# A hybrid attention step on one core: the order in which attention takes its query tiles

## The chip, the core and the metric

The kernel runs on one core of a Trainium2 chip. The core has a matrix engine (TensorE, PE in the profile), a vector engine (VectorE, DVE), a scalar engine (ScalarE, ACT), a general engine (GpSimd, POOL) and a queue engine (SyncE, SP) that issues most transfers (DMA). Each runs its own list of instructions in order and waits on semaphores for the others. [...] The metric is device time in microseconds (us); lower is better.

## The reference, cut to what matters

One layer reads 1024 prompt rows, 64 sample rows and 16 meta rows, all 1024 wide. After a normalisation and one input projection, two attentions run side by side, A over a sliding window and B over the keys that an indexer selects; both are gated, summed, and followed by an output projection and an MLP.

```python
o_a = swa_prompt(qa, ka, va, mk_a, mv_a, attn_sinks, slopes_a)      # branch A: window of 128, whole 64-row chunks
o_b = dsa_prompt(qb, qi, wi, kb, vb, ki, mk_b, mv_b, slopes_b, n)   # branch B: top 256 of all earlier keys
mix = (sigmoid(g_a) * o_a + sigmoid(g_b) * o_b) @ w_o
x = x + rms_norm(mix, g_post_mix)
hid = square(relu(rms_norm(x, g_pre_mlp) @ w_up))
y = x + rms_norm(hid @ w_down, g_post_mlp)
```

Each query row is independent of the others once the keys, values and selections are there, so the order of the query rows is free.

## The kernel before

The program runs in stages with a barrier between them: normalisation and projection (to about 616 us of the span), attention (about 617 to 1103), output projection (to about 1235), MLP (to the end). Queries, gates, the distance masks of branch B and the merged rows pass through scratch tensors in memory.

Attention takes nine query tiles: 0 to 7 are 128 prompt rows each, 8 (`SAMPLE_TILE`) is the 64 sample rows. `ORDER` is the order of the tiles. A tile has two sections, branch A then branch B (`SECTIONS`), a section has two blocks of 64 rows (the sample one), and a block has eight units, one for each pair of heads. So a prompt section has 16 units and a sample section 8. In this text 7A is branch A of tile 7, 0B branch B of tile 0, and SA and SB are the sample's two sections.

The key columns of a unit depend on branch and block (`key_columns`). Branch A: 80 for block 0, 144 for block 1, 208 for every other block and for the sample. Branch B: 80 and 144 for tile 0, 208 and 272 for tile 1, then 64 more for each block, 976 and 1040 for tile 7, and 1104 for the sample. The columns are cut into key tiles of 128; the last is ragged (16 or 80 rows in B, and 17 or 81 in A, where the sink is one column more).

TensorE goes through the units in a software pipeline. In step u it transposes unit u-2 (L1432), computes the scores of unit u+1 (L1418: two passes, the high and low part of the keys) and multiplies unit u-3 by the values (L1446). VectorE adds the distances and finds the minimum (L1357), ScalarE takes the exponential (L1317), both copy the transposes (L1311, L1369), and VectorE normalises four units at a time (L1376, L1383).

The queries of section s+1 are split into a high and a low part by GpSimd (`split_queries`, L1266 and L1269) once section s-1 has been scored and the queries have landed; only section 0 is split by ScalarE and VectorE. SP issues in order: the queries of the first two sections (L1186), the masks of the first two blocks (L1195), their gates (L1203), thirteen output copies (L1218), and then in a loop over the sections the queries two sections ahead, the masks, the stores of merged rows (L1208), the gates and a piece of `w_o` (L1250). Since all loops run over `SECTIONS`, `BLOCK_ORDER` and `ALL`, every engine's list follows `ORDER`.

Of the kernel before, what the change touches and what calls it, by code (L numbers as in the profile page):

```python
# [22 lines left out]
SAMPLE_TILE = 8  # L23
# [1023 lines left out]
def attention(nc, top, c, ps, kv, wo_raw, wo_loaded, w_o, q_scr, gate_scr, dist_scr, merged_scr, t_scr, caches, outs):  # L1047


    with ExitStack() as ctx:  # L1050
        sb = lambda n, s, d=F32: ctx.enter_context(nc.sbuf_tensor(n, s, d))
        sem = lambda n: top.enter_context(nc.semaphore(n))

        ORDER = list(range(SAMPLE_TILE - 1, -1, -1)) + [SAMPLE_TILE]
        SECTIONS = [(t, branch) for t in ORDER for branch in range(2)]
        halves = lambda t: 2 if t < SAMPLE_TILE else 1
        BLOCK_ORDER = [(t, e) for t in ORDER for e in range(halves(t))]
        block_index = {at: i for i, at in enumerate(BLOCK_ORDER)}
# [116 lines left out]
        with nc.Block() as block:  # L1175

            @block.sync
            def _(sp):
# [55 lines left out]
                for s in range(len(SECTIONS)):  # L1234
# [3 lines left out]
                    if branch == 0:  # L1238
                        mine = [i for i, (t, _) in enumerate(BLOCK_ORDER) if t == ORDER[j]]
                        if j >= 1:  # L1240
# [17 lines left out]
            def _(pool):  # L1258
# [13 lines left out]
                def gate_a(i):  # L1272

                    pool.wait_ge(normed, last_quad[i, 0] + 1)
                    pool.wait_ge(gates_loaded[i % 2], 32 * (i // 2 + 1))
                    if i >= 2:
                        pool.wait_ge(merged_stored[i % 2], 32 * (i // 2))
                    pool.tensor_tensor(merged[:, i % 2], mixed[:, 0, i % 2], gates[:, i % 2, 0], ALU.mult).then_inc(gated_a, 1)
                    pool.wait_ge(gated_a, i + 1)
# [9 lines left out]
                for s in range(len(SECTIONS)):  # L1289
# [6 lines left out]
                    if branch == 1:  # L1296
                        for e in range(halves(ORDER[j])):
                            gate_a(2 * j + e)
# [690 lines left out]
def streaming_step(nc, a, o):  # L1989
# [9 lines left out]
    with ExitStack() as top:  # L1999
# [9 lines left out]
        with ExitStack() as mixers:  # L2009
            ctx = ExitStack()  # L2010
            xT = [ctx.enter_context(nc.sbuf_tensor(n, [P, KT, N_TOK], F32R)) for n in ("xT_hi", "xT_lo")]
            b2 = weight_buffers(ctx, nc, weights)
            input_norm(nc, top, c, xT, b2, ws, ps, a["w_in"], a["x_prompt"], a["x_sample"], a["meta_tokens"], a["g_pre_mix"])
            b2 |= projection_buffers(ctx, nc)
            sel = selection_buffers(ctx, nc)


            ctx.close()
            kv = attention_buffers(mixers, top, nc)
            with ExitStack() as ctx:  # L2020
                raw = operand_buffers(ctx, nc)
                projection(nc, top, c, xT, b2, ws, sel, kv, raw, ps, a["w_in"], caches, a["cache_ki_b"], a["attn_sinks"],
                           t_scr, q_scr, gate_scr, dist_scr)
            attention(nc, top, c, ps, kv, wo_raw, wo_loaded, a["w_o"], q_scr, gate_scr, dist_scr, merged_scr, t_scr, caches, o)
# [35 lines left out]
```

## Time and profile before

| | us |
|---|---|
| median of 3 runs | 2064.34 (2063.37 to 2066.57) |
| the profiled execution | 2057.04 |
| its span, first to last instruction | 2055.2 |
| TensorE busy | 1936.7 (94%) |
| VectorE, ScalarE, GpSimd busy | 1185.1, 715.9, 577.3 |
| mean granted clock of TensorE | 0.965 |

The times within the trace are microseconds from the start of the span. The profiled execution lies 1.84 us above its span and 7.30 us below the median of the runs. [...]

### The profile page before, as it was taken

The numbers are of one execution on the slowest core, as the hardware profiler recorded it, in microseconds if no ns is written. First come the engines' busy times: TensorE is split into PE (matmuls) and PEld (weight loads), VectorE is DVE, ScalarE is ACT, GpSimd is POOL, SyncE is SP. The second block draws the span as 40 slices with busy tenths as digits, with TensorE's granted clock in tenths as the row PEclk, the third lists the DMA queues.
The fourth block names the chain that finished last, engine by engine and source line by source line (L and its number), as shares of the span: only waits on it lengthen the run. The fifth ranks groups of instructions, "written<-read, shape, count | busy, mean of one in ns | idle before, by whom it ended". The sixth has DMA issues, their size and how long they took to land. (4 is left out here: it accounts for less than half of the span.)

```text
span 2055.2 us, 31223 instructions
## 1 busy us (share of the span) xinstructions
PE 1936.7 (94%) x11175; PEld 1745.9 (85%) x11175; DVE 1185.1 (58%) x2717; ACT 715.9 (35%) x1408; POOL 577.3 (28%) x444
## 2 busy tenths in 40 slices
PE   4999999999957999999997998999999999999995
PEld 3989999877747999999997877888888888888884
DVE  6028999999885576667754653333333333333337
ACT  5235444233224555556544333111121212121222
POOL 2225554233123123333631002222222222222224
PEclk9999999999976999999968998999999999999998
DMA  5333333333149044445432323111111111111104
GB/s 150 109 84 98 93 94 86 90 101 89 44 110 175 24 85 97 89 89 97 86 75 98 123 82 98 42 41 41 41 41 41 46 41 46 41 46 41 54 12 153
DMA packets 141257, 158.99 MB, mean 77 GB/s; under 512 B 28320, under 2 KB 109296, under 8 KB 141152
## 3 DMA queue, kind: packets, MB, share of 16 engines
q1 hardware_dynamic: 127328, 136.88, 25.2%
q10 hardware_dynamic: 13824, 20.75, 4.3%
q8 instruction: 62, 1.02, 0.2%
q14 instruction: 43, 0.35, 0.1%
HBM read 119.44 MB, written 39.27 MB: 77 GB/s over the span
## 5 line engine op out<-in xcount | busy, mean ns | idle before, releaser
L1962 PE MATMUL ps<-x2T_hi,weights 128*128 128x362 f32 (+1 forms) x1536 | 383.1, 329 | 5.3 <-DVE weights L1928 5.3
L1980 PE MATMUL ps<-weights,hid_hi 128*128 128x512 f32 (+1 forms) x1152 | 363.0, 396 | 0.0
L1913 DVE TENSOR_TENSOR total<-total,ps 128x512 f32<-128x512 f32 (+1 forms) x270 | 184.6, 686 | 164.4 <-PE ps L1980 163.5
L1962 PEld LDWEIGHTS ps<-x2T_hi,weights 128*128 128x128 f32 x1536 | 273.4, 189 | 7.0 <-DVE weights L1928 5.5
L1980 PEld LDWEIGHTS ps<-weights,hid_hi 128*128 128x128 f32 (+1 forms) x1152 | 209.6, 182 | 57.0
L1962 PE MATMUL ps<-x2T_lo,weights 128*128 128x362 f32 (+1 forms) x768 | 252.7, 329 | 0.0
L1898 DVE TENSOR_TENSOR hidden<-hidden 128x362 f32<-128x362 f32 (+1 forms) x96 | 51.5, 537 | 310.7 <-ACT hidden L1871 310.7
L1980 PE MATMUL ps<-weights,hid_lo 128*128 128x512 f32 (+1 forms) x576 | 228.1, 396 | 0.0
L722 DVE MATCH_REPLACE8 score<-top,score 128x1024 f32<-128x1024 f32 (+6 forms) x224 | 207.2, 929 | 0.0
L718 DVE MAX8 top<-score 128x8 f32<-128x1024 f32 (+6 forms) x224 | 203.0, 936 | 1.9
L1831 POOL TENSOR_TENSOR weights<-down_raw,weights 128x512 fp32r<-128x512 f32 x64 | 82.8, 1294 | 419.2 <-ACT weights L1862 419.2
L1317 ACT ACTIVATE probs<-probs,neg 128x209 f32<-128x209 f32 (+19 forms) x272 | 168.8, 622 | 14.3 <-DVE neg L1357 12.1
L1311 ACT ACTIVATE pt<-ps 128x512 f32<-128x512 f32 (+3 forms) x224 | 104.6, 489 | 197.1 <-PE ps L1432 196.7
L1446 PE MATMUL ps<-v_b_p,pt 128*128 128x65 f32 (+2 forms) x1280 | 172.9, 278 | 0.0
L1446 PEld LDWEIGHTS ps<-v_b_p,pt 128*128 128x128 f32 (+2 forms) x1280 | 166.8, 196 | 5.7
L1823 POOL TENSOR_TENSOR weights<-up_raw,weights 128x256 fp32r<-128x256 f32 x124 | 88.2, 747 | 287.7 <-ACT weights L1853 287.7
L1432 PE MATMUL ps<-ident,probs 128*128 128x128 f32 (+2 forms) x976 | 164.5, 288 | 0.2 <-ACT probs L1317 0.2
L782 PE MATMUL ps<-xT_hi,w_hi 128*128 128x362 f32 (+1 forms) x480 | 159.0, 331 | 0.0
L782 PE MATMUL ps<-xT_hi,weights 128*128 128x362 f32 (+1 forms) x480 | 157.6, 328 | 0.0
L782 PE MATMUL ps<-xT_lo,w_hi 128*128 128x362 f32 (+1 forms) x480 | 157.2, 328 | 0.0
L1862 ACT ACTIVATE weights<-down_raw 128x512 fp32r<-128x512 f32 x64 | 40.1, 626 | 318.4 <-PE ps L1980 318.3
L591 POOL TENSOR_TENSOR weights<-w_raw,w_hi 128x512 fp32r<-128x512 f32 x72 | 93.4, 1297 | 200.4 <-ACT w_hi L497 200.2
(189 smaller groups left out, 3604.7 us busy)
## 6 DMA issues: line engine op xcount, KB each, us to landing
w_raw<-in_w_in ACTq DMA_DIRECT2D x72, 256.0 KB, 2.9
q_raw<-q_scr SPq DMA_DIRECT2D x32, 512.0 KB, 8.5
up_raw<-in_w_up SPq DMA_DIRECT2D x64, 256.0 KB, 2.9
down_raw<-in_w_down SPq DMA_DIRECT2D x64, 256.0 KB, 2.6
gates<-gate_scr SPq DMA_DIRECT2D x34, 256.0 KB, 4.7
x_in<-in_x_prompt SPq DMA_DIRECT2D x16, 512.0 KB, 4.8
gate_scr<-stage SPq DMA_DIRECT2D x32, 256.0 KB, 3.0
q_scr<-stage SPq DMA_DIRECT2D x40, 181.0 KB, 3.1
```

The source lines that it names most:

```text
L591: pool.tensor_tensor(w_lo[:, ch % 2, k, 0:w], w_raw[:, n % RAW, 0:w], w_hi[:, ch % 2, k, 0:w].bitcast(F32), ALU.subtract).then_inc(w_lo_do ...
L718: dve.max(top8[:tile_rows(INDEX_TILES[i]), i % 2], works[i]).then_inc(select_step[i % 2], 1)
L722: dve.match_replace(works[i], top8[:tile_rows(INDEX_TILES[i]), i % 2], works[i], TAKEN)\
L782: last = pe.matmul(out, a, b, start=(k == 0 and j == 0), stop=(k == KT - 1 and j == 2))
L1311: act.activation(pt[:, u % PT, a:a + n, :], src, ACT.Copy).then_inc(copied_act, 1)
L1317: act.activation(probs[:, u % 3, 0:w], probs[:, u % 3, 0:w], ACT.Exp, bias=neg[:, branch, h:h + 1], scale=-1.0).then_inc(exped, 1)
L1432: last = pe.transpose(ps[0:rows, T_BANK + x % 3, b * P:(b + 1) * P], probs[:, u % 3, col:col + rows], c["ident"][:])
L1446: last = pe.matmul(out_bank(q)[:, a, :], pt[0:rows, u % PT, j, :], values(u, j, rows), start=(j == 0), stop=(j == len(tiles) - 1))
L1823: pool.tensor_tensor(up_lo[:, k, :], up_raw[:, k // 2, k % 2, :], up_hi[:, k, :].bitcast(F32), ALU.subtract).then_inc(up_lo_done, 1)
L1913: dve.tensor_tensor(out, out, ps[:r, UP_BANKS + g % DOWN_BANKS, :], ALU.add).then_inc(added, 1)
L1962: last = pe.matmul(ps[:, g % UP_BANKS, 0:n], a[:, k, fs], b, start=(k == 0 and i == 0), stop=(k == KT - 1 and i == 2))
L1980: last = pe.matmul(ps[:r, UP_BANKS + g % DOWN_BANKS, :], a, b[:, f, cols], start=(f == 0 and i == 0), stop=(f == FT - 1 and i == 2))
```

## The change

One line changes: tiles 0 and 1 go first, then 7 down to 2, then the sample.

```diff
-        ORDER = list(range(SAMPLE_TILE - 1, -1, -1)) + [SAMPLE_TILE]
+        ORDER = [0, 1] + list(range(SAMPLE_TILE - 1, 1, -1)) + [SAMPLE_TILE]
```

The sections were 7A 7B 6A 6B ... 2A 2B 1A 1B 0A 0B SA SB, and are 0A 0B 1A 1B 7A 7B ... 2A 2B SA SB. No instruction is added or removed.

TensorE at the start of attention, before (L1418 scores, L1432 transposes by `ident`, L1446 values):

```order
L1404 UNCONDITIONAL_BRANCH
L1418 MATMUL ps<-k_a_p,q_st 128x208 x6
L1432 MATMUL ps<-ident,probs 128x128
L1432 MATMUL ps<-ident,probs 81x128
L1418 MATMUL ps<-k_a_p,q_st 128x208 x2
```

TensorE at the same place, after:

```order
L1404 UNCONDITIONAL_BRANCH
L1418 MATMUL ps<-k_a_p,q_st 128x80 x6
L1432 MATMUL ps<-ident,probs 81x128
L1418 MATMUL ps<-k_a_p,q_st 128x80 x2
L1432 MATMUL ps<-ident,probs 81x128
```

The first units now have 80 key columns and one key tile where they had 208 and two.

TensorE where the sample begins (`k_a_s` are its keys of branch A), before:

```order
L1418 MATMUL ps<-k_b_p,q_st 128x144 x2
L1446 MATMUL ps<-v_b_p,pt 128x65 x2
L1432 MATMUL ps<-ident,probs 128x128
L1432 MATMUL ps<-ident,probs 16x128
L1418 MATMUL ps<-k_a_s,q_st 128x208 x2
```

TensorE where the sample begins, after:

```order
L1418 MATMUL ps<-k_b_p,q_st 128x400 x2
L1446 MATMUL ps<-v_b_p,pt 128x65 x4
L1432 MATMUL ps<-ident,probs 128x128 x3
L1432 MATMUL ps<-ident,probs 16x128
L1418 MATMUL ps<-k_a_s,q_st 128x208 x2
```

The sample now follows the second block of tile 2 (400 columns, four key tiles) where it followed that of tile 0.

SP after the thirteen output copies, in the change from before (-) to after (+); the rows above this piece are the queries of sections 2 and 3:

```order
 L1186 DMA q_raw<-q_scr 64x16x128 x4
+L1195 DMA dist_b<-dist_scr 64x208 x2
+L1195 DMA dist_b<-dist_scr 64x272 x2
+L1208 DMA merged_scr<-merged 64x512 x4
+L1203 DMA gates<-gate_scr 64x1024 x4
+L1250 DMA wo_raw<-in_w_o 64x1024 x2
+L1186 DMA q_raw<-q_scr 64x16x128 x4
+L1195 DMA dist_b<-dist_scr 64x976 x2
+L1195 DMA dist_b<-dist_scr 64x1040 x2
```

The masks of tile 1 are loaded where those of tile 6 stood; all transfers keep their kind and their place in the loop.

## Rows read from the trace of the kernel before

**Rows 1.** The page: 40 slices of the span, TensorE busy and its granted clock.

```profile
PE   4999999999957999999997998999999999999995
PEclk9999999999976999999968998999999999999998
```

**Rows 2.** Stretches of attention, all engines: length, busy time, clock, DMA.

```profile
core 0: us, PE busy (x) PEld busy (x) DVE busy (x) ACT busy (x) POOL busy (x), PEclk, DMA share, GB/s
630.36:655.37 25.01, 24.76 (x118) 24.20 (x119) 14.73 (x64) 9.43 (x23) 8.26 (x3) 0.50 0.92 191
657.00:980.88 323.88, 323.88 (x2688) 314.37 (x2687) 211.74 (x767) 186.45 (x339) 109.52 (x54) 1.00 0.43 81
980.88:997.91 17.03, 17.03 (x151) 16.38 (x149) 13.73 (x62) 9.51 (x24) 10.59 (x7) 1.00 0.40 94
997.91:1014.66 16.75, 16.75 (x146) 15.90 (x144) 12.59 (x51) 11.03 (x26) 9.62 (x5) 1.00 0.88 138
1014.66:1029.64 14.98, 14.66 (x117) 13.25 (x115) 11.59 (x64) 8.07 (x25) 11.21 (x7) 1.00 0.29 63
1032.30:1050.91 18.61, 18.61 (x87) 16.78 (x86) 8.46 (x43) 6.96 (x21) 3.86 (x5) 0.50 0.51 97
1050.91:1065.23 14.32, 14.32 (x66) 13.22 (x65) 7.20 (x32) 4.67 (x12) 7.40 (x5) 0.50 0.19 44
1065.23:1101.00 35.77, 35.30 (x286) 34.23 (x284) 19.70 (x65) 18.31 (x26) 1.27 (x1) 0.98 0.05 13
```

**Rows 3.** Waits of TensorE from 640 to 1101: total, times, longest.

```profile
PE ps L1418 <- DVE neg L1357: 0.4, 2, 0.2
PE ps L1446 <- ACT pt L1311: 0.2, 1, 0.2
```

**Rows 4.** Stretches, score matmuls (L1418) alone, two for each unit: length, busy, clock.

```profile
634.97:649.37 14.40, 6.61 (x18) 4.91 (x19) 0.50 0.78 167
988.43:997.07 8.64, 4.54 (x20) 3.02 (x21) 1.00 0.61 144
998.75:1004.08 5.33, 2.72 (x12) 1.81 (x13) 1.00 1.13 198
1010.21:1013.17 2.96, 0.99 (x4) 0.59 (x5) 1.00 0.04 6
1020.07:1022.91 2.84, 2.00 (x10) 1.50 (x11) 1.00 0.00 0
1026.27:1028.51 2.24, 0.85 (x4) 0.60 (x5) 1.00 0.81 145
1035.84:1038.72 2.88, 1.88 (x6) 1.64 (x7) 0.50 1.10 143
1044.97:1050.90 5.93, 2.04 (x6) 1.64 (x7) 0.50 0.01 3
```

**Rows 5.** Timeline of TensorE where the clock rises: start, length, instruction.

```profile
655.37 1.87 PE L1418 MATMUL ps<-k_b_p,q_st 128*128 128x488 f32 x4
657.61 1.13 PE L1418 MATMUL ps<-k_b_p,q_st 128*128 128x488 f32 x4
...
1065.23 1.85 PE L1418 MATMUL ps<-k_b_s,q_st 128*128 128x368 f32 x6
...
1072.55 1.34 PE L1418 MATMUL ps<-k_b_s,q_st 128*128 128x368 f32 x6
```

**Rows 6.** Stretches at the end of projection, where TensorE only transposes keys.

```profile
605.30:608.90 3.60, 3.58 (x16) 3.27 (x17) 1.54 (x3) 0.75 (x1) 0.00 (x0) 0.50 0.27 51
609.20:611.10 1.90, 1.90 (x17) 1.74 (x16) 1.31 (x3) 0.20 (x1) 0.00 (x0) 1.00 0.61 136
```

**Rows 7.** Timelines of GpSimd and SP at the start of attention.

```profile
645.07 1.36 SPq L1186 DMA_DIRECT2D q_raw<-q_scr  x2
...
653.52 1.89 POOL L1266 CAST q_st<-q_raw 128x2048 fp32r<-128x2048 f32 x1 [15.19 <-DMA q_raw<-q_scr]
655.49 4.58 POOL L1269 TENSOR_TENSOR q_st<-q_raw,q_st 64x2048 fp32r<-64x2048 f32 x1
```

## The prediction, made before the changed kernel had run

> **What bounds the kernel now.** I first read the page's 40 slices [rows 1]. TensorE is nine tenths busy in nearly all of them, and its clock is full except in three places. Slices 12 to 14 and 21 to 22 are the two ends of attention, where the change acts. I then cut attention into stretches by the first score of each section [rows 2]. From 657 to 1101 TensorE has work in the pipeline almost without a gap, and the list of its waits there sums to 0.6 us [rows 3]. VectorE is busy for 12 to 15 us of each prompt section of 15 to 17, ScalarE and GpSimd less. So attention costs what TensorE's instructions cost, and these are the same before and after. The order can only change two things: at which clock each section runs, and whether something arrives late.
>
> The reader is to see the clock column of [rows 2]. It is 0.50 in 7A (630.36 to 655.37), 1.00 from 657 on through 1A, 1B and 0A, 0.50 from 1032.30 through most of 0B and all of SA, and full again in SB. In 7A TensorE is marked busy for 24.76 of 25.01 us, so it is not idleness that keeps the clock low there, and at 1032.30 the clock fell although there was no gap in the rows. The work is what differs. Prompt sections of branch A with 208 columns stay at whichever level they find: 7A at the low one for 25 us, 1A at the high one for 17 [rows 2]. Only the dense score runs of a wide branch B lift the clock: four matmuls of 488 columns at 655.37 and six of 368 at 1065.23, both of which started slow and were followed by fast ones (1.87 us, then 1.13; 1.85 us, then 1.34) [rows 5].
>
> **What one unit costs at either clock** [rows 4]. A stretch there holds a whole number of pipeline steps, two score matmuls each.
> - 208 columns (two key tiles): low clock 14.40 / 9 = 1.60 us; high clock 8.64 / 10 = 0.864 in branch A and 5.33 / 6 = 0.888 in branch B.
> - 80 columns (one tile): low 2.88 / 3 = 0.96; high 2.84 / 5 = 0.57.
> - 144 columns (one tile and a ragged one): low 5.93 / 3 = 1.98; high 2.24 / 2 = 1.12.
> - 272 columns (two tiles and a ragged one): high 2.96 / 2 = 1.48. The low clock isn't shown. From below it is the 1.98 of one tile less, from above twice 1.48 = 2.96. I take 1.98 plus the step from one tile to two at the low clock (1.60 - 0.96 = 0.64), so 2.62.
> The low price of 80 and 144 columns was seen in 0B, and I use it for 0A too, where the second branch-A unit differs by one column (81, 145).
>
> **The change part by part.** The start is as now: SP issues the same queries first, TensorE begins at about 630 at the low clock. What follows now is 0A, 0B, 1A, 1B, 7A, and the first dense score run comes with 7B. So I expect the low clock from the start to the beginning of 7B.
> - 0A moves from the high to the low clock: 8 x (0.96 - 0.57) + 8 x (1.98 - 1.12) = 3.1 + 6.9 = +10.0.
> - 0B was low in all but its first 2.7 us and stays low. The values of 0A's last units trail into those microseconds, and I have charged them to 0A. Nothing more: 0.
> - 1A moves to the low clock: 16 x (1.60 - 0.864) = +11.8.
> - 1B moves to the low clock: 8 x (1.60 - 0.888) + 8 x (2.62 - 1.48) = 5.7 + 9.1 = +14.8. By the bounds of the 272-column step the second part is 8 x (1.98 - 1.48) = 4.0 to 8 x (2.96 - 1.48) = 11.8.
> - 7A was low and stays low: 0.
> - SA now follows the 400-column block of tile 2 at the high clock, as 1A did before, and so stays high: 8 x (0.864 - 1.60) = -5.9. If it fell to the low clock all the same, this term would be 0.
> - SB's first score run is fast: 1.34 - 1.85 = -0.5.
> - The pipeline fills with narrower units: at most 1.60 - 0.96 = 0.64, I take -0.5.
> - 7B's first microseconds: the rise came 1.5 us after its first dense run began, and may come later at another moment. Between 0 and +1.6; I take +0.5.
>
> Sum: 10.0 + 11.8 + 14.8 - 5.9 - 0.5 - 0.5 + 0.5 = +30.2. The profiled execution would go from 2057.0 to 2087.2. The runs' median is 7.3 above the profiled execution for before, and I carry the same difference: 2064.3 + 30.2 = 2094.5.
>
> **What could arrive late.** The queries of 1A are section 2's, and their load is issued behind the thirteen output copies, at 645.07; GpSimd begins their split at 653.52 and is done at 655.49 + 4.58 = 660.07 [rows 7]. Its condition, the scores of section 0 done, comes at about the same time in the new order: 630.4 + 8 x 0.96 + 8 x 1.98 = 653.9. 1A is wanted at about 630.4 + 2 x 23.5 = 677.4, so 17 us remain. For each later section GpSimd begins the split when the section before last has been scored, and needs 6.5 us where the shortest section lasts 23.5. The masks of tiles 0 and 1 are narrower than those of tile 7, so fewer bytes are moved at the start. The stores of tile 0 and the gates of tile 1 stand in front of section 5's queries in SP's list, and those are needed only after 1A and 1B, two sections later. I cost all of it at nothing. What hides it is the slower clock itself; if one section's queries did come late, each microsecond would be one of an idle TensorE.
>
> [...] The row shows 7A at 0.50 for 25.01 us with TensorE busy throughout [rows 2]. [...] A second row shows TensorE with nothing but transposes of keys: 16 in 3.60 us at 0.50, and right after them 17 in 1.90 us at 1.00 [rows 6]. [...]
>
> **The rivals.**
> 1. *The clock rises at the start of 1A*, when the 208-column units follow the small ones. Then 1A and 1B cost what they do now, 7A becomes fast, and only 0A is charged: 10.0 - 11.8 (7A, 16 x 0.736) - 5.9 - 0.5 - 0.5 = -8.7, so 2055.6, faster than before. It decides if 1A differs for the clock from 7A, which has units of the same form and stayed low for all 16. Nothing speaks for it but the alignment of the moment. 5 in 100.
> 2. *The clock rises in 1B*, with the 272-column block or a little before. At the start of 1B: -8.7 + 11.8 = +3.1 (2067.4); at its second block: +5.7 more, +8.8 (2073.1). For it: 272 columns is the widest run before 7A. Against it: such a step has 544 score columns in 2.62 us, and a 208 step 416 in 1.60, so at the low clock it is the thinner one. 7 in 100.
> 3. [...] 3 in 100.
> 4. *The queries or gates come late*. The split of section 2 has 17 us to spare; beyond them each microsecond adds one to the 30.2. With a wait of 5 to 10 us: 2100 to 2105. 4 in 100.
> 5. *The order doesn't matter*, because SA falls to the low clock and something I don't see lifts it in 1A: within a few microseconds of before. 1 in 100.
>
> **How the numbers follow.** My forecast has 80 in 100. Its own range: the 272-column step gives -5.1 to +2.7, the rise in 7B -0.5 to +1.1, and the runs of before lie within 3.2 us of each other, so about 2088 to 2101. For 8 times in 10 I go from 2085 to 2102, which takes in the low end of the 272-column step with some error of the measurement, and leaves out the rivals 1 to 3. A measurement of this kernel can tell about 0.2%, 4 us, from no change. Faster by more: rivals 1 and 3, 0.08. Within it: half of rival 2 and rival 5, 0.05. Slower: the rest, 0.87.
>
> **What would show it.** The stretches of the changed profile should have the clock at 0.50 from about 630 to about 763 (630.4 + 23.5 + 23.5 + 25.6 + 12.8 + 21.0 + 25.6 = 762.4), and at 1.00 without a break from there to the end of SB. Attention should end about 30 us later, at some 1131 instead of 1101, and output projection and MLP should be shifted but not changed. Steps of 80, 144 and 208 columns should have the low prices named, and the first rows of 272 columns at the low clock should be 2.6 us apart. The forecast is wrong if the clock is at 1.00 anywhere before 7B, if SA is at 0.50, or if TensorE has a wait of more than a microsecond on queries (L1269) or masks after its first score.

## The result: 0.3% slower, where 1.5% slower was forecast

| | us |
|---|---|
| changed kernel, median of 12 runs | 2069.52 (2065.84 to 2071.8) |
| before, median of 12 runs beside it | 2064.14 (2055.53 to 2066.57) |
| ratio | 1.0032, 95% interval 1.0019 to 1.0046 |
| forecast | 2094.5, range 2085 to 2102 |

The sign was right. The rise forecast was +30.2 us and the medians differ by 5.4. The changed kernel's profiled execution took 2069.63 us (span 2067.9), against 2057.04 for the one of before: +12.6. That these two differences are not the same is half of the story below.

The slices of the changed kernel's page answer to [rows 1]:

```profile
PE   4999999999958999999997997999999999999995
PEclk7999999999975599999998998999999999999998
```

The low clock at the end of attention is gone, and the one at its start is longer. The same cut by first scores as in [rows 2], with the columns named there, for 0A, 0B, 1A, then 1B in three pieces, 7A, and at the end 2B and SA:

```profile
629.98:648.45 18.47, 18.46 (x85) 17.00 (x85) 10.83 (x60) 7.72 (x23) 6.42 (x2) 0.50 0.89 179
648.45:671.88 23.43, 23.43 (x106) 20.96 (x105) 10.08 (x49) 7.96 (x24) 10.07 (x5) 0.50 0.67 113
671.88:699.01 27.13, 27.13 (x131) 26.03 (x129) 14.45 (x64) 9.53 (x24) 11.06 (x7) 0.50 0.62 122
699.01:711.81 12.80, 12.80 (x67) 12.63 (x65) 6.19 (x25) 4.78 (x13) 8.26 (x4) 0.50 0.48 84
711.81:717.40 5.59, 5.59 (x29) 5.46 (x28) 2.84 (x10) 1.65 (x5) 0.00 (x0) 0.50 0.35 90
717.50:724.24 6.74, 6.74 (x53) 6.10 (x52) 4.08 (x15) 3.83 (x9) 0.83 (x1) 0.98 0.01 2
724.24:740.17 15.93, 15.93 (x142) 15.28 (x139) 13.52 (x62) 9.53 (x24) 10.94 (x7) 1.00 0.36 84
1044.40:1066.59 22.19, 22.19 (x183) 21.53 (x182) 15.63 (x52) 13.48 (x26) 6.83 (x6) 1.00 0.39 77
1066.59:1076.68 10.09, 10.09 (x88) 9.51 (x85) 7.16 (x30) 4.44 (x12) 7.41 (x5) 1.00 0.13 28
```

The clock is 0.50 through 0A, 0B, 1A and the first block of 1B, as forecast, and SA is at full clock (10.09 us, 14.32 before), as forecast. But it rises at 717.8, in the second block of 1B (0.50 up to there, 0.98 as the mean of the stretch from 717.50), and 7A runs at full clock. The steps there show what was overlooked. TensorE's timeline of the changed kernel (start, length, instruction):

```profile
711.81 0.80 PE L1418 MATMUL ps<-k_b_p,q_st 128*128 128x272 f32 x2
712.40 0.95 PE L1446 MATMUL ps<-v_b_p,pt 128*128 128x65 f32 x4
713.15 0.63 PE L1432 MATMUL ps<-ident,probs 128*128 128x128 f32 x2
713.43 0.80 PE L1418 MATMUL ps<-k_b_p,q_st 128*128 128x272 f32 x2
...
715.06 0.80 PE L1418 MATMUL ps<-k_b_p,q_st 128*128 128x272 f32 x2
715.66 0.95 PE L1446 MATMUL ps<-v_b_p,pt 128*128 128x65 f32 x4
716.40 0.84 PE L1432 MATMUL ps<-ident,probs 128*128 128x128 f32 x3
716.90 0.80 PE L1418 MATMUL ps<-k_b_p,q_st 128*128 128x272 f32 x2
717.50 0.70 PE L1446 MATMUL ps<-v_b_p,pt 128*128 128x65 f32 x4
718.03 0.50 PE L1432 MATMUL ps<-ident,probs 128*128 128x128 f32 x3
718.29 0.51 PE L1418 MATMUL ps<-k_b_p,q_st 128*128 128x272 f32 x2
```

The scores run ahead: in the first two steps of the block there are 272 score columns and still the transposes and values of the 208-column units, with two key tiles. Such a step takes 713.43 - 711.81 = 1.62 us. The third has three transposes but still the values of two tiles, and takes 716.90 - 715.06 = 1.84 us. The clock rose in the fourth. The forecast had the first rows of 272 columns 2.6 us apart, the price of a full step, and called that step the thinner one.

Nothing came late. The changed kernel's waits of TensorE from 640 to 1112 answer to [rows 3], and GpSimd had 1A's queries split at 656.04, 15.8 us before 1A's first score (17 forecast; [rows 7]):

```profile
PE ps L1418 <- DVE neg L1357: 0.4, 2, 0.2
PE ps L1418 <- DVE neg_part L1357: 0.2, 1, 0.2
```

```profile
649.56 1.90 POOL L1266 CAST q_st<-q_raw 128x2048 fp32r<-128x2048 f32 x1 [11.69 <-DMA q_raw<-q_scr]
651.53 4.51 POOL L1269 TENSOR_TENSOR q_st<-q_raw,q_st 64x2048 fp32r<-64x2048 f32 x1
```

### The profile page after: what moved, and what is told of

Its sections match the earlier page's. It is cut to its first block and busy times, and to the rows that moved or that the text cites. A ratio compares the mean times of both kernels' runs of the same rounds, so it can differ in the third digit from the quotient of the medians.

```text
span 2067.9 us, 31223 instructions
## 1 busy us (share of the span) xinstructions
PE 1950.1 (94%) x11175; PEld 1758.0 (85%) x11175; DVE 1187.2 (57%) x2717; ACT 716.2 (35%) x1408; POOL 577.7 (28%) x444
## 5 line engine op out<-in xcount | busy, mean ns | idle before, releaser
L1446 PE MATMUL ps<-v_b_p,pt 128*128 128x65 f32 (+2 forms) x1280 | 175.5, 281 | 0.0
L1446 PEld LDWEIGHTS ps<-v_b_p,pt 128*128 128x128 f32 (+2 forms) x1280 | 170.2, 199 | 5.6
L1432 PE MATMUL ps<-ident,probs 128*128 128x128 f32 (+3 forms) x976 | 168.8, 293 | 0.0
```

The source lines that it names most:

```text
L1432: last = pe.transpose(ps[0:rows, T_BANK + x % 3, b * P:(b + 1) * P], probs[:, u % 3, col:col + rows], c["ident"][:])
L1446: last = pe.matmul(out_bank(q)[:, a, :], pt[0:rows, u % PT, j, :], values(u, j, rows), start=(j == 0), stop=(j == len(tiles) - 1))
```

## The experiments

Two theories stood at first. C: all of the difference is TensorE's clock. M: the new order, or the runs of before that take longer than its profile, cost in another way. In 12 runs, 9 of before took 2063 to 2067 us and 3 took 2055 to 2057, and its profile was one of the short ones.

### The kernel before, profiled twice more

No edit.

> The kernel before, unchanged, for a second profile. Its first profile took 2057.0 us, while 9 of 12 runs of it took about 2064 and 3 about 2056. Theory C (all of it is TensorE's clock, and the clock does not fall at the same place in every run): a run of about 2064 has 20 us or so more at granted clock 0.50 in attention than the first profile, by an earlier fall in 1B or 0A (before 1032), since a microsecond at the low clock costs about 0.4. Rival M (the 8 us lie in the MLP or in the projection): attention is as in the first profile, 470.6 us from its first score to 1101, and another stage is longer.

> The kernel before, unchanged, once more. Its times come in groups of about 2044, 2056 and 2065. Theory C: the group follows from two independent events, whether the clock rises early in 7A (low for 25 us or for about 6) and whether it falls early in 0A (near the first 80-column units) or only in 0B. A run of about 2065 has both losses: 7A at 0.50 for 25 us and the fall at the start of 0A; 2044 has neither; about 2056 has one. Rival M: a run of 2065 has the clock of the first profile and a longer MLP or projection.

Measured: 2054.58 and 2065.36 us. The first is again a short one, so only the second tests what a run of about 2065 looks like. The 19 runs of before in the first series were 3 between 2044 and 2051, 5 between 2054 and 2057, and 11 between 2063 and 2068. Stretches of the execution of 2065.36: 7A, the start of 7B, on to 0A, the start of 0A, the rest of 0A with 0B, and SA.

```profile
630.24:652.45 22.21, 21.96 (x108) 21.71 (x109) 12.54 (x59) 9.25 (x23) 6.43 (x2) 0.50 0.93 192
652.45:655.00 2.55, 2.55 (x11) 2.24 (x10) 1.96 (x6) 0.18 (x1) 1.08 (x1) 0.50 1.02 216
655.10:1013.78 358.68, 358.68 (x2983) 347.58 (x2982) 238.98 (x880) 208.28 (x388) 131.92 (x65) 1.00 0.46 86
1013.78:1020.20 6.42, 6.33 (x51) 5.66 (x48) 4.12 (x20) 2.33 (x8) 6.26 (x3) 1.00 0.08 14
1020.30:1058.25 37.95, 37.95 (x172) 34.16 (x172) 18.38 (x94) 13.87 (x41) 11.26 (x10) 0.50 0.41 85
1058.25:1072.58 14.33, 14.33 (x67) 13.23 (x65) 7.22 (x32) 4.67 (x12) 7.40 (x5) 0.50 0.22 45
```

The clock fell at 1020.4, 6.6 us after 0A's first score; in the profile of [rows 2] it fell 17.7 us after (1014.66 to 1032.4). 0A and 0B together took 1058.25 - 1013.78 = 44.5 us here and 1050.91 - 1014.66 = 36.3 there. That is +8.2 of the 8.3 by which this execution is longer than the first profiled one. It had 37.95 - 18.61 = 19.3 us more at 0.50, so one such microsecond cost 0.42 us here, where about 0.4 was expected. And the execution of 2054.58, from its first score on:

```profile
628.48:633.90 5.42, 5.17 (x24) 4.92 (x25) 3.25 (x18) 2.58 (x7) 3.87 (x2) 0.50 1.04 246
634.00:643.00 9.00, 9.00 (x86) 8.92 (x85) 8.30 (x40) 6.33 (x16) 2.47 (x1) 1.00 0.84 182
643.00:1003.09 360.09, 360.09 (x2994) 348.87 (x2992) 240.90 (x887) 208.97 (x390) 133.16 (x65) 1.00 0.48 90
1003.09:1009.40 6.31, 6.31 (x50) 5.62 (x47) 4.02 (x20) 2.22 (x8) 6.15 (x3) 1.00 0.08 14
1009.50:1047.73 38.23, 38.23 (x171) 34.45 (x172) 18.47 (x94) 13.96 (x42) 11.39 (x10) 0.50 0.42 85
```

Here the clock rose 5.5 us after the first score, within 7A, and fell early in 0A. This execution is 10.8 us shorter than the one of 2065.36: 9.0 of them lie in 7A and 7B (66.95 us from 7A's first score to 6A's, against 75.92), and 1.8 in a first score that came earlier (628.48, against 630.24), which is not the clock. So two events vary from run to run: an early or late rise in 7A, and an early or late fall in tile 0. Theory C has the groups: both losses in the profiled 2065.4, one in the profiled 2054.6 and 2057.0. No run near 2046 was profiled, so that these have neither is not shown. From SB's first score to the end of the span the three take 990.0, 990.8 and 991.0 us, so rival M, by which a later stage is longer, does not explain the difference of some 8 to 11 us.

### Extra matmuls ahead of the first score

```diff
+                for _ in range(56):
+                    pe.matmul(ps[:, 7, :], kv["k_b_p"][:, 0, 0:P], kv["k_b_p"][:, 0, 16:528], start=True, stop=True)
                 score(0)
```

> The kernel before with 56 extra matmuls of 512 columns on TensorE (their result is never read) ahead of the first score, in the 14 us in which TensorE waits for the first queries. Theory C (7A costs 25 us because it starts at the low clock): the clock is 1.00 when the first scores start, 7A takes about 13.6 us where it took 25.0, and the time falls by 11 to 12 us against before, with the rest as before. Rival M (the low speed of 7A comes from the transfers and the start of the pipeline, not from the clock): 7A stays at 24 to 25 us and the time is the same or a few us longer, for the extra matmuls.

Measured: 2053.39 us, ratio 0.9954 (0.9925 to 0.9983), 10.6 between the medians. The extra matmuls, and then the start of 7A:

```profile
615.16:628.05 12.89, 12.89 (x56) 10.41 (x56) 2.29 (x1) 3.20 (x2) 0.00 (x0) 1.00 1.06 173
628.09:642.00 13.91, 13.26 (x117) 12.86 (x117) 12.79 (x62) 9.66 (x23) 6.45 (x2) 1.00 0.96 216
```

7A took 12.6 us, from 628.09 to 7B's first score at 640.69, and ran at full clock under a DMA share as high as in [rows 2]. Its slowness was the clock, not the transfers. The clock then fell 6.8 us into tile 0 (1007.6, first score at 1000.80), as early as in the two profiles above. The 10.6 us lie just under the 11 to 12 expected.

### The changed kernel with the same matmuls

The edit is the one above, made in the changed kernel.

> The changed kernel with only the 56 matmuls ahead of the first score. Theory C: the clock is 1.00 at the start, falls early in 0A or in 0B, is 0.50 through 1A and rises in the second block of 1B as in the changed kernel; at most the 10 us of 0A are won, so 2059 to 2069, and it stays above before_warm (2053.4). Rival D (once the clock is up at the start it stays up): about 2040.

Measured: 2061.89 us, ratio to before 1.0020 (0.9989 to 1.0050). Three stretches, up to the fall, to the rise, and on:

```profile
628.00:648.60 20.60, 19.82 (x143) 17.54 (x141) 14.99 (x78) 10.79 (x32) 6.42 (x2) 1.00 0.91 176
648.80:710.10 61.30, 61.30 (x293) 58.39 (x293) 31.22 (x132) 22.66 (x58) 29.38 (x14) 0.50 0.67 125
710.20:1100.00 389.80, 389.17 (x3218) 376.30 (x3217) 257.83 (x942) 223.49 (x407) 130.02 (x67) 1.00 0.38 74
```

The high clock of the start did not last through tile 0 in the profiled execution: it fell at 648.7, in 0B, with no gap of TensorE over 0.13 us in the ten microseconds before. It was won back at 710.1, in the fifth step of 1B's second block, whose first score came at 702.47. Theory C held, within its wide range; rival D (about 2040) fell.

### The 272 score columns cut in two

```diff
-            n = -(-w // 512)
+            n = 2 if w == 272 else -(-w // 512)
```

> The changed kernel, but the 272 score columns of the second block of 1B are cut into two pieces of 136, which doubles the weight loads and VectorE's instructions for these 8 units and changes nothing else. Theory C (in the changed kernel the clock rises in this block because of its scores of 272 columns, before its own transposes and values come): the clock stays at 0.50 until 7B, 7A takes 25 us again, and the time goes up by 13 to 20 us against the changed kernel, to some 2083 to 2090. Rival D (the clock rises there for another reason, such as the number of units done or the time since the last idleness): it rises in 1B as in the changed kernel, and the time is 2070 to 2073.

Measured: 2093.43 us, ratio to before 1.0169 (1.0122 to 1.0216), 23.9 above the changed kernel. Score matmuls alone in 1B's two blocks, 7A, and 7B before and after the rise:

```profile
699.57:712.37 12.80, 5.86 (x16) 4.36 (x17) 0.50 0.49 84
712.37:733.09 20.72, 8.80 (x33) 7.79 (x33) 0.50 0.10 25
733.09:762.34 29.25, 11.75 (x32) 8.74 (x33) 0.50 0.63 126
762.34:765.50 3.16, 2.33 (x5) 1.56 (x6) 0.50 0.00 0
765.60:785.19 19.59, 7.70 (x28) 4.49 (x28) 1.00 0.32 55
```

With the same columns in smaller pieces the clock did not rise in 1B, stayed low through 7A and rose in 7B, 3.3 us after its first score. I had expected 13 to 20 us over the changed kernel; 7A alone is 29.25 - 15.93 = +13.3, 1B is (733.09 - 699.57) - (724.24 - 699.01) = +8.3. All four runs lie between 2092.5 and 2093.7, and all twelve of the changed kernel between 2065.8 and 2071.8. So the rise in 1B, profiled once, is very likely no accident of that execution.

Not all of the 23.9 us is the clock, for the pieces cost something too. The second block took 20.72 / 8 = 2.59 us a step, but that is a mean of light and full steps. TensorE's timeline has the first two scores of the block, and two where all of the step belongs to 272-column units:

```profile
712.37 1.10 PE L1418 MATMUL ps<-k_b_p,q_st 128*128 128x136 f32 x4
714.40 1.10 PE L1418 MATMUL ps<-k_b_p,q_st 128*128 128x136 f32 x4
...
720.90 1.10 PE L1418 MATMUL ps<-k_b_p,q_st 128*128 128x136 f32 x4
723.95 1.10 PE L1418 MATMUL ps<-k_b_p,q_st 128*128 128x136 f32 x4
```

A first step takes 2.03 us where the whole one took 1.62, so the cut costs 0.4 us a unit, some 3 us for eight. A full step takes 3.05; less 0.4, that makes an estimate of 2.65 for a full step with its scores in one piece.

The clock is as in the forecast here, and 2093.4 was measured where 2094.5 was forecast. That the two are so near is partly luck: by the profiles the rise is 2093.67 - 2057.04 = +36.6 us (+33.4 without the pieces) where +30.2 was forecast, and the 7.3 us from profile to median, which the forecast added, are not there (2093.67 and 2093.43).

The cut was made in all eight units. So it shows that the scores of this block in one piece bring the rise, and not which of its steps do; for the first steps speaks only that the clock rose in the fourth step in one profile and in the fifth in the other.

### Tile 0 alone first

```diff
+        ORDER = [0] + list(range(SAMPLE_TILE - 1, 0, -1)) + [SAMPLE_TILE]
```

> Half of the change: tile 0 alone goes first, then 7 down to 1, then the sample. Theory C: the clock is 0.50 through 0A, 0B and 7A and 1.00 from 7B to the end. Against the first profile of before (2057.0): +10.0 for 0A, -5.9 for SA, -1.0 for the first scores, so about +3, 2060; against runs of before of 2064, -4. Tile 1 is charged nothing, so this beats the whole change (2069.5) by 5 to 10 us. Rival M (small tiles at the head cost by themselves, by late queries, masks or gates): TensorE shows waits of more than a microsecond in 0B or 7A, and the time is 2064 or more.

Measured: 2062.53 us, ratio 1.0013 (0.9986 to 1.0040): no measurable difference from before, and 7.0 below the changed kernel, so that tile 1's move costs about that. Its profiled execution (2063.05) is 6.0 above the first of before, where about 3 was expected. TensorE's waits are 0.6 us, so rival M finds nothing here. The clock is 0.50 from the start until 2.1 us after 7B begins (701.15, first score at 699.04), and full from there to the end of attention:

```profile
630.02:671.92 41.90, 41.89 (x188) 37.94 (x189) 20.89 (x108) 15.68 (x47) 16.48 (x7) 0.50 0.80 151
671.92:699.04 27.12, 27.12 (x130) 26.02 (x129) 14.45 (x64) 9.52 (x24) 11.05 (x7) 0.50 0.66 136
```

### Fillers in tile 0, in both orders

Beside the 56 matmuls ahead, one more before the scores of each unit of tile 0, with the same 512 key columns, into the bank that the scores then overwrite:

```diff
+                        if t == 0:
+                            pe.matmul(ps[:, x % 3, :], q, kv["k_b_p"][:, 0, 16:528], start=True, stop=True)
                         for part in range(2):
```

> The kernel before with the 56 matmuls of before_warm, and one more matmul of 512 columns in front of the scores of each of the 32 units of tile 0 (its result is overwritten by the scores). It works more than the kernel before: 32 x 0.23 = 7.4 us of TensorE. Theory C (the clock falls in tile 0 because its steps have few columns): with the fillers the clock stays at 1.00 from the start of attention to its end, and against the first profile of before (2057.0) the sum is -11.4 (7A) -10.0 (0B) -5.9 (SA) -0.5 +7.4 = -20, so about 2037; against before_warm (2053.4) -12 to -17. Rival D (the fall has another cause than the thin steps): the clock falls in 0A or 0B as in before_warm, and the time is 2055 to 2061.

> The changed kernel with the same two additions. Theory C (the order of the tiles costs by the clock alone): with the clock at 1.00 throughout attention the order has nothing left to act on, and the time is that of before_fill within 2 us, about 2037. Rival M (the new order costs something besides, such as late queries, masks or gates at the faster clock): it is 4 us or more above before_fill, with waits of TensorE on L1269 or L1357 in 0B to 7A.

Measured: 2038.61 us (ratio 0.9909, 0.9880 to 0.9938) and 2037.76 us (0.9898, 0.9865 to 0.9932). They are some 25 us faster than before and 31 faster than the changed kernel, with more work. Most of attention with the fillers, first in the old order, then in the new one:

```profile
615.00:1080.00 465.00, 462.16 (x3750) 442.45 (x3751) 304.41 (x1152) 260.99 (x500) 165.92 (x83) 1.00 0.48 91
```

```profile
622.00:1080.00 458.00, 457.37 (x3732) 438.79 (x3730) 303.30 (x1151) 260.57 (x498) 165.96 (x83) 1.00 0.47 90
```

With the clock at 1.00 from the first score to the end of attention, the two orders lie 0.9 us apart, and about 2037 was expected for both. From the first score to SB's first it is 415.2 us in the old order (629.86 to 1045.10) and 414.2 in the new (630.86 to 1045.04). So, to within about 1 us, the order acts by the clock alone. Rival M and rival D fell.

## Why the prediction was wrong, step by step

- *Attention is TensorE's instructions and its clock; nothing comes late.* Right: the waits are the same 0.6 us, and the filler runs leave no other cost over 1 us.
- *0A, 0B, 1A and 1B's first block go to the low clock; SA to the high one.* Right. The low prices were right too: 0.96, 1.60 and 1.98 us came back between full steps of 80, 208 and 144 columns. The unseen full step of 272 columns, taken as 2.62, is 2.65 by the estimate above; with its scores in one piece and at the low clock, no run shows one.
- *"1B moves to the low clock", "7A was low and stays low".* This step failed. The clock rose 6.0 us into 1B's second block. That block was charged +9.1 and took +2.7 (12.43 us, and 9.74 before, from 1004.92 to 1014.66); 7A was charged nothing and took -6.3 (15.93 us, and 22.21 before). I had weighed a full 272-column step, and not the first steps of the block, where the scores run ahead of their own transposes and values; yet dense score runs were what I named for the rises in 7B and SB. Cutting these scores in two undid the rise; the time went up by 23.9 us, some 3 of them for the pieces. Rival 2, with 7 in 100, had the place, and +8.8 against the profiled +12.6. It let the clock rise at the block's first score; the three steps before the rise took 5.09 us (711.81 to 716.90), and 2.82 at full clock in the kernel before (1004.92 to 1007.74), which is 2.3 us of the rest.
- *The base.* I took the profile's 2057.0 as typical and carried 7.3 us to the median. In the profiled 2065.36 such us were the clock too: it falls early in 0A. So for the typical run of before I charged 0A some 8 us that it already paid. That is about the difference between +12.6 by profiles and +5.4 by medians. Of the 24.8 us by which the forecast was too high, 17.6 are thus in the rise by profiles (30.2 and 12.6), 12.7 of them by the failed step (9.1 - 2.7 + 6.3), and 7.2 in the base. Against the profiled 2065.36 the changed kernel's is +4.3, and the first score of 0A or 7A to the first score of SB grew from 442.3 (1072.58 - 630.24) to 446.7 us (1076.68 - 629.98), +4.4.
- *"Sections with 208 columns stay at whichever level they find."* Too strong. It held in the profile I had; in another execution of the same kernel the clock rose 5.5 us into attention, among units of 208 columns.
- *A boundary misread.* I took 655.37 for 7B's first score. The timeline of before has an earlier one, below, so 7A is 22.2 us long (652.57 - 630.36), not 25.0, and the rise came over 4 us after the dense run began, not 1.5. The sum used steps, so it did not change. Nor is it right that there was no gap before the fall at 1032.3: the longest in the 20 us before it is 0.24 us, at 1023.3. It hardly speaks against the reading: the clock stayed at 1.00 for 9.0 us after it, and in the filler run of before it stays at 1.00 across three gaps of 0.21 us between 1047 and 1051.

```profile
652.57 1.97 PE L1418 MATMUL ps<-k_b_p,q_st 128*128 128x488 f32 x4
```

- *The third rival, 3 in 100: the clock rises shortly after the start and stays.* It did not, and no run shows that a busy TensorE is enough for it. The changed kernel had TensorE busy for 81.82 of the 81.83 us from 629.98 to 711.81, all of them at 0.50, and with the extra matmuls the clock fell at 648.7 with no gap over 0.13 us in the ten microseconds before. Of the kernel before, the execution of 2054.58 had a rise 5.5 us after the first score, and that of 2065.36 none in the 24.8 us from 630.24 to 655.00.

## What to carry to other kernels

Where TensorE has no waits and its clock is still at 0.50, look at single steps of the pipeline and not only at units: a software pipeline mixes the new unit's scores with the old unit's values, and here the clock rose among the first five steps of such a block, which decided it for all of 7A. A time that comes in groups may hide an event that falls either way, so profile one execution of each group before a difference is charged to the change. And where the low clock is the bound, adding work can gain more than reordering it: here 56 idle-time matmuls and 32 fillers, about 7 us of paid work (32 x 12.89 / 56, an estimate from the extra matmuls' rate), won some 25.

## What the runs showed of the hardware

- The same instruction list had its clock rise at 634.0 or only after 655, and fall 6.4 or 17.7 us into tile 0, from one execution to the next: runs from 2044 to 2067 us.
- The 16 units of 7A kept a granted clock of 1.00 in the changed kernel and took 15.93 us; in before they sat at 0.50 and took 22.21 us. TensorE was marked busy for 15.93 and 21.96 us of these, so the longer time shows as busy time and not as gaps.
- Cutting a matmul's moving columns from 272 to two of 136, in 8 units of 272, kept the clock down for 48 us more (717.8 to 765.6).
- The clock fell among units of 80 and 144 columns with no gap of TensorE over 0.24 us in the ten microseconds before (1032.4, 1020.4, 1009.5, 1007.6 and 648.7 us in five executions), and one more matmul of 512 columns before each of these units' scores kept it at 1.00 in two executions.
